# VectorE turns an expert's activations in 32x32 blocks in place of TensorE and ACT copies, and the expert's second set begins in another PSUM bank

## The reference

```python
# layer 0: differential attention and sliding-window attention side by side, then a dense SwiGLU (D_FF 2816)
# layer 1: multi-head latent attention, then top-2-of-8 experts, each a SwiGLU of width 3584
def swiglu(h, w_gu, w_down):
    g, u = jnp.split(h @ w_gu, 2, axis=-1)
    return (jax.nn.silu(g) * u) @ w_down

def moe_swiglu(h, w_router, w_gu, w_down):
    logits = (h @ w_router).astype(jnp.float32)
    vals, idx = lax.top_k(logits, TOP_K)
    gates = jax.nn.softmax(vals, axis=-1)
    combine = jnp.sum(jax.nn.one_hot(idx, N_EXPERTS, dtype=jnp.float32) * gates[..., None], axis=-2)
    y = jnp.zeros_like(h)
    for e in range(N_EXPERTS):
        y = y + combine[..., e:e + 1].astype(h.dtype) * swiglu(h, w_gu[e], w_down[e])
    return y
```

## Time and profile before

| | |
|---|---|
| median of 3 runs | 1286.14 us |
| the runs | 1285.27, 1286.14, 1287.65 us |
| span of the profiled execution | 1286.1 us |
| its own time | 1286.1 us by the profile; no other time is given for it |
| PE busy | 1241.9 us, 97% |
| VectorE (DVE) busy | 466.2 us, 36% |
| ACT busy | 356.3 us, 28% |
| read from HBM | 411.0 MB |

### The profile page before, as it was taken

One profiled execution on the slowest core, in us unless ns is written; L12 is line 12 of the kernel. 1 busy time (PEld: TensorE's weight loads), 2 busy tenths in 40 slices (PEclk: granted clock), 3 DMA queues, 4 the chain that ended last, 5 costly groups with the idle time before them and its releaser, 6 DMA issues.

```text
span 1286.1 us, 22093 instructions
## 1 busy us (share of the span) xinstructions
PE 1241.9 (97%) x9506; PEld 614.2 (48%) x9506; DVE 466.2 (36%) x840; ACT 356.3 (28%) x727; POOL 60.7 (5%) x87
## 2 busy tenths in 40 slices
PE   8978999999979999999999999999999999999998
PEld 6757888888768623343333343333343333334332
DVE  5967656556755511221221132132122122311212
ACT  7465554554865200120100120011120010102101
POOL 4300000000610000000000000000000000000000
PEclk9989999999998999999999999999999999999998
DMA  9403555544502799999999999999999999999995
GB/s 346 180 16 129 193 177 190 190 168 140 197 6 99 316 370 386 378 370 422 420 420 419 421 420 421 421 419 408 420 421 421 420 420 420 421 421 412 399 420 226
DMA packets 58664, 413.56 MB, mean 322 GB/s; under 512 B 6848, under 2 KB 6992, under 8 KB 9280
## 3 DMA queue, kind: packets, MB, share of 16 engines
q1 hardware_dynamic: 57744, 411.20, 79.4%
q0 software_dynamic: 528, 0.79, 0.5%
q10 hardware_dynamic: 288, 0.08, 0.0%
HBM read 411.00 MB, written 1.05 MB: 320 GB/s over the span
## 4 chain that ended last, share of the span: by engine, by line
PE 90%; DVE 4%; ACT 4%; issue 1%; DMA 1%; SPq 0%; ACTq 0%; DVEq 0%
PE PS L2254 39%; PE PS L2262 20%; PE PS L1742 7%; PE PS L1744 6%; PE PS L1743 6%; PE PS L2156 2%; PE PS L2134 2%; PE PS L2204 2%; PE PS L1855 2%; PE PS L1810 1%; DMA ring<-in_dense_tiles 1%; DVE w_lo L1105 1%; ACT arena L715 1%; PE PS L1763 1%; ACT w_hi L672 1%
## 5 line engine op out<-in xcount | busy, mean ns | idle before, releaser
L2254 PE MATMUL PS<-homes,arena 128*32 128x512 f32 x4704 | 516.0, 593 | 4.8 <-DVE arena L1663 4.8
L2254 PEld LDWEIGHTS PS<-homes,arena 128*32 128x32 f32 x4704 | 150.1, 110 | 345.4 <-issue 338.0
L2262 PE MATMUL PS<-homes,arena 128*32 128x512 f32 x2016 | 222.4, 593 | 0.0
L1652 DVE SCALAR_TENSOR_TENSOR arena<-arena,PS 64x512 f32<-64x512 f32 x48 | 32.6, 680 | 437.9 <-ACT arena L1037 437.9
L1742 PE MATMUL PS<-w_hi,hT_hi 128*128 128x512 f32 (+2 forms) x372 | 142.1, 382 | 7.1 <-DVE w_lo L1105 5.1
L1744 PE MATMUL PS<-w_hi,hT_lo 128*128 128x512 f32 (+2 forms) x372 | 139.4, 375 | 0.0
L1743 PE MATMUL PS<-w_lo,hT_hi 128*128 128x512 f32 (+2 forms) x372 | 139.2, 374 | 0.0
L2262 PEld LDWEIGHTS PS<-homes,arena 128*32 128x32 f32 x2016 | 64.7, 110 | 146.9 <-issue 145.9
L1024 ACT ACTIVATE arena<-PS 128x512 f32<-128x512 f32 x24 | 14.3, 597 | 350.2 <-PE PS L2204 350.2
L1037 ACT ACTIVATE arena<-PS 64x512 f32<-64x512 f32 x63 | 37.2, 591 | 253.1 <-PE PS L2254 253.1
L1105 DVE SCALAR_TENSOR_TENSOR w_lo<-ring,gains,w_hi 128x512 fp32r<-128x512 f32 (+3 forms) x152 | 98.6, 712 | 22.5 <-ACT w_hi L672 22.4
(11 more groups left out here) (223 smaller groups left out, 953.7 us busy)
## 6 DMA issues: line engine op xcount, KB each, us to landing
homes<-in_expert_tiles SPq DMA_DIRECT2D x336, 1024.0 KB, 16.3
ring<-in_dense_tiles SPq DMA_DIRECT2D x49, 1024.0 KB, 4.8
ring<-in_dense_tiles SPq DMA_DIRECT2D x6, 512.0 KB, 6.7
ring<-in_dense_tiles SPq DMA_DIRECT2D x2, 832.0 KB, 4.2
x_res<-in_x SPq DMA_DIRECT2D x2, 512.0 KB, 4.2
out<-x_res SPq DMA_DIRECT2D x4, 256.0 KB, 2.9
ring<-in_dense_tiles SPq DMA_DIRECT2D x2, 256.0 KB, 7.2
rope<-in_rope POOLq DMA_DIRECT2D x2, 72.0 KB, 7.8
```

The source lines that it names most:

```text
L1652: v.scalar_tensor_tensor(out=act_of[g], in0=gate[0:64, g, :], scalar=1.0, in1=PS[0:64, g, :], op0=ALU.add, op1=ALU.mult).then_inc(half_sil ...
L2254: ins = pe.matmul(PS[GROUP * q:GROUP * (q + 1), g, :], xT[:, cc, o + g * GROUP:o + (g + 1) * GROUP], w[:, q * COLS:(q + 1) * COLS], start= ...
L2262: ins = pe.matmul(PS[GROUP * q:GROUP * (q + 1), 3 + g, :], tokens_T(k, c, q // 2, g), w[:, q * COLS:(q + 1) * COLS], start=k == 0 and c == ...
```

## The change

What it does, in four parts:

1. `transpose_acts` and its ACT copies go. VectorE turns each group's activations by one `transpose` instruction (`turn`), which transposes every 32x32 block by itself: 128 x 256 values for sets 0 to 2, 128 x 128 for set 3. In each set it comes after `silu_second` of the same group, one group later in VectorE's order.
2. So that the turned blocks are what the down matmuls need, all groups are now laid as the third was: `silu_first` and `silu_second` are two instructions of 64 x 256 for every group, L1699 becomes four of 32 x 128, and the rows of the down weights are stored in another order in HBM (same sizes). `act_T` has two buffers, for even and odd sets.
3. Set 1 uses PSUM banks 6, 0, 1 in place of 0, 1, 2 for its gu sums. Its first group waits for nothing, the second for the first group of set 0, the third for the second.
4. A d piece with c = 0 waits for `aT_ready` group by group. The wait for `scat_added` ahead of the old transposes goes; the gather after the third piece of d 2 waits for `set3_added`.

```diff
+GU_BANKS = ((0, 1, 2), (6, 0, 1), (0, 1, 2), (0, 1, 2))
+def bank_user(k, g, ng):
+    uses = [(kk, gg) for kk in range(k) for gg in range(ng) if GU_BANKS[kk][gg] == GU_BANKS[k][g]]
+    return uses[-1] if uses else None
...
+        act_T = (arena2[:, 5632:6400].rearrange("p (g n) -> p g n", g=NG),
+                 arena1[:, 2560:3328].rearrange("p (g n) -> p g n", g=NG))
+        act_exp = arena2[:, 4864:5632].rearrange("p (g n) -> p g n", g=NG)
...
-                    copy_acts(per_set * k, aT_pair, 6)
-                    if ng == 3:
-                        copy_third(per_set * k + 1)
...
+            def silu_first(k, g):
                 for j in range(2):
+                    c = slice(256 * j, 256 * (j + 1))
+                    ins = v.scalar_tensor_tensor(out=act_exp[64 * j:64 * (j + 1), g, :], in0=gate[0:64, g, c], scalar=1.0,
+                                                 in1=PS[0:64, GU_BANKS[k][g], c], op0=ALU.add, op1=ALU.mult)
                 ins.then_inc(half_silu, 1)
+            def silu_second(k, g):
                 for j in range(2):
+                    half, c = act_exp[64 * j:64 * (j + 1), g, :], slice(256 * j, 256 * (j + 1))
+                    ins = v.scalar_tensor_tensor(out=half, in0=half, scalar=0.5, in1=PS[64:P, GU_BANKS[k][g], c],
                                                  op0=ALU.mult, op1=ALU.mult)
                 ins.then_inc(act_ready, 1)
...
+                def turn(k, g, n):
+                    v.wait_ge(act_ready, per(ab + ng * k + g + 1, e, 4 * NG))
+                    v.transpose(act_T[k % 2][:, g, 0:n], act_exp[:, g, 0:n]).then_inc(aT_ready, 1)
+                def turned(k):
+                    if p or i or k:
+                        v.wait_ge(aT_ready, per(4 * gb + ng * k, e, 4 * NG))
                 for k in range(SETS):
-                    for g in range(ng + 1):
+                    turned(k)
+                    for g in range(ng + 2):
                         if g < ng:
                             v.wait_ge(gate_ready, per(hb + ng * k + g + 1, e, 4 * NG))
+                            silu_first(k, g)
+                        if 0 < g <= ng:
                             v.wait_ge(half_silu, per(hb + ng * k + g, e, 4 * NG))
+                            silu_second(k, g - 1)
+                        if g > 1:
+                            turn(k, g - 2, 256)
...
+                        for j in range(4):
+                            c = slice(P * j, P * (j + 1))
+                            ins = v.scalar_tensor_tensor(out=act_exp[GROUP * j:GROUP * (j + 1), g - 1, 0:P],
+                                                         in0=aux[GROUP:64, g - 1, c], scalar=0.5,
+                                                         in1=gate[GROUP:64, g - 1, c], op0=ALU.mult, op1=ALU.mult)
...
             def tokens_T(k, m, j, g):
+                b = 2 * m + j
+                return act_T[k % 2][:, g, GROUP * b:GROUP * (b + 1)]
...
                             if c == 0:
-                                before = ng * (k - 1) + g + 1 if k or p or not i else \
-                                    min(g + 1, GROUPS_AT[i - 1]) - GROUPS_AT[i - 1]
-                                pe.wait_ge(act_ready, per(ab + before, e, 4 * NG))
+                                user = bank_user(k, g, ng)
+                                if user:
+                                    before = ng * user[0] + user[1] + 1
+                                elif k == 0 and (p or i):
+                                    before = 0 if p else min(g + 1, GROUPS_AT[i - 1]) - GROUPS_AT[i - 1]
+                                else:
+                                    before = None
+                                if before is not None:
+                                    pe.wait_ge(act_ready, per(ab + before, e, 4 * NG))
...
                         else:
+                            if c == 0:
+                                pe.wait_ge(aT_ready, per(4 * gb + ng * k + g + 1, e, 4 * NG))
...
-                    if kind == "gu" and k and c == (3 if k < SETS else 1):
-                        if k == 1:
-                            if p or i in SCATTER_AT:
-                                pe.wait_ge(scat_added, per(sb_ + 4, e, 4))
-                        transpose_acts(k - 1)
                     if kind == "d" and k == SETS - 1 and c == CHUNKS_DN - 2:
-                        transpose_acts(SETS)
                         if p == 0 and i in GATHER_AT:
+                            pe.wait_ge(set3_added, gb + ng)
                             pe.wait_ge(onehot_ready, MARKS)
                             gather(i + 1)
```

More of the change, by code:

```diff
@@ L1012, in expert @@
                 ub = U0 + (NE * p + i) * NU
-                gb, tb = groups_before(p, i), transposes_before(p, i)
+                gb = groups_before(p, i)
                 sets_b = 4 * (gb - NE * p - i)
[L1016 to L1025, removed]
                 def set_done(k, g, last):
@@ L1688, in expert @@
                     v.wait_ge(odd_copied, per(gb + g + 1, e, NG))
-                    v.tensor_tensor(gate[0:64, g, :], gate[0:64, g, :], PS[0:64, g, :], ALU.add)\
+                    v.tensor_tensor(gate[0:64, g, :], gate[0:64, g, :], PS[0:64, GU_BANKS[SETS][g], :], ALU.add)\
                         .then_inc(set3_added, 1)
-                for g in range(ng + 1):
+                turned(SETS)
+                for g in range(ng + 2):
                     if g < ng:
@@ L1696, in expert @@
                             .then_inc(half_silu, 1)
[L1697 removed]
+                    if 0 < g <= ng:
                         v.wait_ge(half_silu, per(hb + ng * SETS + g, e, 4 * NG))
[L1699 to L1701 removed]
+                        for j in range(4):
[3 more added lines that the diff above has]
+                                                         in1=gate[GROUP:64, g - 1, c], op0=ALU.mult, op1=ALU.mult)
+                        ins.then_inc(act_ready, 1)
+                    if g > 1:
+                        turn(SETS, g - 2, P)
                 for n in range(2):
@@ L2181, in tokens_T @@
             def tokens_T(k, m, j, g):
[L2183 to L2189 removed]
+                b = 2 * m + j
+                return act_T[k % 2][:, g, GROUP * b:GROUP * (b + 1)]
             def expert(p, i, e, ng, last):
[L2192 removed]
+                gb, sb_ = groups_before(p, i), scatters_before(p, i)
                 ab = X_ACT + 4 * gb
[L2195 to L2210 removed]
                 if p:
@@ L2228, in expert @@
                     if kind == "d" and c == 0:
-                        pe.wait_ge(aT_ready, per(tb + (ng - 1) * min(k + 1, SETS) + (k == SETS), e, 7))
                         if k == 0 and p:
@@ L2289, in expert @@
                         elif p and not last:
+                            pe.wait_ge(set3_added, per(gb + ng, e, NG))
                             gather_loop(e + 1)
@@ L2371, in expert_tiles @@
         if kind == "d":
-            r = k * 1024 + c * 2 * P
-            tiles[:, n] = down[:, r:r + 2 * P].reshape(NE, P, PIECE)
+            r = k * 1024
+            if k < SETS:
+                rows = down[:, r:r + 1024].reshape(NE, 2, 2, 8, GROUP, D).transpose(0, 3, 2, 1, 4, 5)
+            else:
+                rows = down[:, r:r + COLS].reshape(NE, 4, 4, GROUP, D).transpose(0, 2, 1, 3, 4)
+            rows = rows.reshape(NE, -1, P, D)[:, 2 * c:2 * c + 2]
+            tiles[:, n] = rows.transpose(0, 2, 1, 3).reshape(NE, P, PIECE)
         elif k < SETS:
```

68 lines of the change are left out of this document (5 added, 63 removed).

## The result

| | before | after |
|---|---|---|
| median | 1286.89 us (4 runs) | 1276.88 us (4 runs, 1274.64 to 1277.92) |
| ratio | | 0.9921, 95% interval 0.9905 to 0.9938 |
| span of the profiled execution | 1286.1 us | 1276.1 us |

The change makes the kernel 10 us (0.8%) faster, 8 to 12 by the interval, where 5.5 were forecast. Two further series of the same kernel gave 0.9924 and 0.9918. The profiled execution after took 1277.92 us by its own time, 1.8 more than its span; of the first runs before, 1287.65 us lies about as far above the profiled span and is probably that execution. The prediction took the span for the own time and for the median; this enters the times before and after alike and leaves the forecast gain of 5.5 as it is.

A forecast was written before the change was run, and what follows sets the result against it. TensorE was taken to bind until about 563 us, the transfers after; 3.9 + 0.3 us bring landings 4.2 us sooner, and the last piece starting on landing plus an 11.8 us tail gives median 1280.6 us, 8-in-10 range 1277.5 to 1285.3.

The forecast's parts named there:

- What bounds the kernel: Experts: TensorE sets the pace from 443 to 563 us, the transfers from there to 1271.2 at 417 GB/s.
- the border: Near 563 us in the first profile: pieces 54 to 56 are the last to meet an empty queue; piece 56 lands at 568.0.
- Transposes off TensorE: All eight experts: at most 31.7 us off TensorE, of which 3.9 us, early in the experts, moves the end.
- Set 1 in bank 6: First expert, set 0 to set 1: the stall moves to group 2, winning 0.3 us, bounds 0 to 2.0.
- Turning on VectorE: VectorE in the experts: 0.42 us per turn, bounds 0.41 to 0.68, some 58 us more in all, costing nothing.
- The sum: Whole kernel: landings 4.2 us sooner, last piece ends at 1268.9, 11.8 us follow; median 1280.6, 5.5 us less.
- the tail: After the last d matmuls: 11.8 us of adding, scattering and storing, carried over unchanged.
- The term for the end: Last piece, begun 1.4 us after landing before the change: it would start on landing, with 0.15 us to wake.
- A: Experts: the queue could deliver faster, TensorE keeps the pace and the whole 31.7 us shows, 1254 us; 5%.
- B: Last pieces and first scatter pair: granted clock falls to half while TensorE waits, 1284.5 us; 12%.
- D: Waiting stretch at the end: clock falls and stays down, kernel slower than 1288.7, up to 1293 us; 4%.
- C: First expert gives nothing: VectorE waits at set 1 grow 2 us or more, or queue not empty enough; 1283.8 us; 10%.

The follow-up runs named there:

- The loads at the two places: 20 idle matmuls added to the changed kernel, in gu 2 of the first expert or of the sixth: 0.9977 and 0.9936 of the kernel before.
- the small pieces: Both kernels with 7/8 of the bytes of every piece after the first 15: before 1.0004, changed 0.9730 (1250.64 us), each to the kernel before.
- b_again: The kernel before, unchanged, profiled anew: 0.9996 of itself (0.9983 to 1.0008).
- b_drop_first: The kernel before with TensorE's transposes left out in the first expert alone: 0.9963 of the kernel before (0.9950 to 0.9975).
- a_again: The changed kernel, unchanged, run and profiled anew: 0.9924 of the kernel before (0.9909 to 0.9939).
- no_hole_late: The changed kernel with set 1 of first and fifth expert in banks 6, 7, 0, gate buffer guard in set 1's fifth piece: 0.9921 of the kernel before.
- load_first: The changed kernel with 20 idle matmuls in gu 2 of the first expert: 0.9977 of the kernel before (0.9966 to 0.9988).

## Why the prediction was right and wrong

*What bounds the kernel* was right: TensorE ahead of the border, the transfers behind it. The loads at the two places, the unchanged 417 GB/s and the small pieces show it. The waits for landing pieces came in the fifth and the last expert as forecast, 17.1 us where some 20 were forecast, and the last landing came 26.3 us after its issue.

*Transposes off TensorE* was right: 31.7 us at most forecast in all, 30 with the bank's part shown with small pieces. Ahead of the border 3.9 us were forecast; the first expert's sets give the 3 x 1.05 us, but the transposes ahead of its gather only 0.5 where 0.7 was put (piece 39 is that much shorter). *Set 1 in bank 6* was right: the first piece of set 1 loses 1.9 us in place of 2.3, so 0.4 are won where 0.3 were forecast. Together the step to the border was forecast at 4.2 and measured at 3.9.

*Turning on VectorE* was right: 0.42 us forecast, 0.429 measured; for a quarter of the set 3 products 0.28 forecast, 0.282 measured; for the narrow turn 0.3 forecast, 0.296 measured. No wait of TensorE ends with a turn. The Trainium skill's sentence on the block transpose (Vector Engine (DVE) Microarchitecture Reference, section 3.8) agrees with these rows: the turn of 256 columns takes 0.429 us and a product of the same width 0.414.

*The sum* is the step that failed, and in it the tail. The sum carried the tail over as 11.8 us. That was a tail in which the clock had fallen in the last scatter; where it does not, the changed kernel's takes 9.8 to 10.0 us, and over three profiles it averages 10.6 against 12.0 in two before. Filling the hole ahead of that scatter gained 2 us in the kernel before and nothing in the changed one. The term for the end was too small as well. It was 1.3 us, from one profile in which the clock had held; in b_again and b_drop_first, where it fell in the hole of the fifth expert and no later wait absorbed the loss, the last piece ended 4.0 and 4.2 us after its landing, so 2.0 and 2.2 us were to be won. With 3.9 for the border, 1.1 for the transfers (no change was forecast), 1.6 for the end and 1.4 for the tail the profiles show 8 us, where the runs show 10, with 8 to 12 as the interval. The range was too narrow at its low end of 1277.5: it gave the untouched dense part and the tail no room, though rows 3 show the clock at 0.70 over the last stretch. The measured 1276.88 lies 0.6 us below it.

*Rivals*: A (the transfers follow) fell: the rate stayed at 417 GB/s. The Trainium skill (DMA: Bandwidth & Descriptors, section on where 436 GB/s comes from) gives 435 GB/s as the ceiling of the SBUF ports; no run here shows it. B and D (the clock falls while TensorE waits) happened in a_again and no_hole_late, once each in the waits of the fifth expert. There the last piece still ended 2.0 us after its landing. In load_first the clock fell in the last piece, and the tail took 13.3 us. The Trainium skill (TensorE: Matmul & The Clock Gate, section "HAM oscillation") tells of a kernel whose clock fell at every wait for DMA, with waits of some 3 to 5 us. The waits here are mostly 0.55 us on PE, and of eleven profiles with these waits two have a fall in the fifth expert's. C fell: the first expert gave its 3.9.

*Open*: some 2 of the 10 us, beyond the 8 that the profiles show from piece 0 on. They are not the start of the experts, which comes at the same time on average in the profiles of both kernels. Some 3 of the 10 us seem to go with the clock, by a comparison of runs and not by an experiment: the mean granted clock over all runs was 0.988 before and 0.991 after, and among the runs at 0.990 or 0.991 thirteen of the kernel before average 1283.8 us and eight of the changed kernel 1277.2, 6.6 apart. A part of that clock is the tail's, which spent 8.8 and 9.1 us at half clock in the two profiles before and 1.3, 8.6 and 1.9 us after. Where the rest lies was not shown.

## What to carry to other kernels

Where engine and transfers are both near their limit, look for the last transfer that met an empty queue: here work taken off the engine ahead of it moved the end nearly one for one, work behind it only as far as the engine was late at the end. The place holds only as long as the engine keeps up: 5 us more of it in the sixth expert of the kernel before emptied the queue again. Take the tail's clock from the granted clock of its own rows before carrying its length over. And an engine with waits in its stream can absorb later mishaps that a continuously busy one passes on: the clock's fall near 911 us left the end of the last piece at 2.0 us after its landing, the falls near 890 us made it 4.0 and 4.2.

## What the runs showed that was not expected

- Behind the same dense code piece 0 was used between 440.4 and 447.0 us over the nineteen profiles, with 13.7 to 30.7 us of the time before 445 us at the lower clock.
- With the queue long, the issue itself became slow. In before, b_again, after and a_again an issue on SPq took 0.33 to 0.45 us as long as at most eight earlier pieces had not landed, and up to 7.7 us with ten or eleven; at the end of the changed kernel it took 1.99. So the landing 26.3 us after issue is not the whole time that a piece stands in line.
- 20 idle matmuls took 4.7 us on PE and made their piece 4.8 us longer. The idle 0.84 us of the weight loads ahead of them cost nothing of its own, since PE was still at work on the piece before.
